# A quarter of the input projection as seven products of quadrants in one first stage, and a thinner projection beside each attention unit

## The reference

```python
h = rmsnorm(x, norm_w)
qa, ka, va, ga, qb, kb, vb, gb = split(h @ w_in)     # 1024, 1024, 1024, 1024, 1024, 128, 128, 1024 columns
qa, ka = rope(rmsnorm(heads(qa))), rope(rmsnorm(heads(ka)))   # 16 heads of 64 each
# A: 8 units; two causal softmax maps of 1024x1024 each, their difference times v (128 wide)
oa = rmsnorm((softmax(q1 @ k1.T) - lam * softmax(q2 @ k2.T)) @ va) * (1 - lam_init)
# B: 16 query heads on 2 key/value heads, window of 128, a learned sink in each softmax
y = concat(oa * silu(ga), ob * silu(gb))
out = x + y @ w_out
```

## Time and profile before

| | us |
|---|---|
| executions shown, two | 1876.48 and 1877.36 |
| median | 1876.92 |
| profiled execution, span of its core | 1877.2 |
| PE busy | 1807.0 |
| DVE busy | 1109.2 |
| ACT busy | 799.8 |
| POOL busy | 439.0 |

### The profile page before, as it was taken

The page is one execution under the profiler, slowest core; times in us unless marked ns, Lnnn a source line. Parts: engine busy times, 40 slices in busy tenths (PEclk is TensorE's granted clock), DMA queues, the critical chain, the costliest instruction groups (busy, mean ns, idle before and its releaser), DMA issues.

```text
span 1877.2 us, 27880 instructions
## 1 busy us (share of the span) xinstructions
PE 1807.0 (96%) x8920; PEld 1507.0 (80%) x8920; DVE 1109.2 (59%) x2255; ACT 799.8 (43%) x2116; POOL 439.0 (23%) x664
## 2 busy tenths in 40 slices
PE   3899999999999999999999999999999889999999
PEld 3788878888788887888878888888888678788887
DVE  5734465665656657566575666758677866333333
ACT  5411354444544445444444444445444554222221
POOL 6512131322313223131231312313223521000000
PEclk9999999999999999999999999999999889999999
DMA  5122222222222222222222222323323544444445
GB/s 201 36 79 73 84 72 78 78 78 78 71 77 77 77 78 71 85 69 87 68 74 86 73 84 74 105 82 83 109 80 98 189 127 122 162 154 161 142 143 177
DMA packets 256504, 184.97 MB, mean 99 GB/s; under 512 B 31136, under 2 KB 227744, under 8 KB 255392
## 3 DMA queue, kind: packets, MB, share of 16 engines
q1 hardware_dynamic: 254352, 183.85, 32.3%
q10 hardware_dynamic: 2064, 0.01, 0.1%
HBM read 138.71 MB, written 45.09 MB: 98 GB/s over the span
## 4 chain that ended last, share of the span: by engine, by line
PE 79%; DVE 9%; issue 4%; DMA 3%; ACT 2%; POOL 2%; SPq 1%; DVEq 0%; ACTq 0%
PE ps_a L854 19%; PE ps_a L856 19%; PE ps_a L855 19%; PE ps_b L938 3%; PE ps_b L856 3%; PE ps_b L854 3%; PE ps_b L855 3%; PE ps_a L898 2%; DVE stage_rows L1124 2%; DMA qkv_sb<-qkv_a_dram 2%; PE ps_a L897 2%; PE ps_b L953 2%; PE ps_b L891 2%; PE ps_b L984 1%; DVE w_lo_sb L1124 1%
## 5 line engine op out<-in xcount | busy, mean ns | idle before, releaser
L854 PE MATMUL ps_a<-hT_hi,w_hi_sb 128*128 128x512 f32 x1696 | 694.1, 409 | 7.2 <-DVE stage_rows L1208 4.5
L856 PE MATMUL ps_a<-hT_hi,w_lo_sb 128*128 128x512 f32 x1696 | 667.4, 394 | 0.0
L855 PE MATMUL ps_a<-hT_lo,w_hi_sb 128*128 128x512 f32 x1696 | 664.1, 392 | 0.0
L1124 DVE TENSOR_TENSOR w_lo_sb<-w_raw_sb,w_hi_sb 128x512 fp32r<-128x512 f32 (+1 forms) x320 | 228.3, 716 | 272.1 <-ACT w_hi_sb L657 270.1
L856 PEld LDWEIGHTS ps_a<-hT_hi,w_lo_sb 128*128 128x128 f32 x1696 | 320.1, 189 | 71.8
L854 PEld LDWEIGHTS ps_a<-hT_hi,w_hi_sb 128*128 128x128 f32 x1696 | 321.2, 189 | 70.2 <-issue 7.2
L855 PEld LDWEIGHTS ps_a<-hT_lo,w_hi_sb 128*128 128x128 f32 x1696 | 321.8, 190 | 58.5
L657 ACT ACTIVATE w_hi_sb<-w_raw_sb 128x512 fp32r<-128x512 f32 (+1 forms) x320 | 197.8, 620 | 226.4 <-DMA w_raw_sb<-in_w_out 95.0
L817 ACT ACTIVATE expd<-ps_a,neg_max 128x256 f32<-128x256 f32 (+7 forms) x128 | 95.1, 743 | 213.3 <-DVE neg_max L1265 211.4
L749 ACT ACTIVATE attention_parts<-ps_b 128x512 fp32r<-128x512 f32 (+3 forms) x160 | 76.9, 521 | 224.2 <-PE ps_b L938 224.0
L1124 DVE TENSOR_TENSOR ps_a<-ps_a,mask 128x128 f32<-128x128 f32 (+2 forms) x192 | 77.5, 417 | 142.2 <-PE ps_a L898 140.8
(11 more groups left out here) (126 smaller groups left out, 2651.6 us busy)
## 6 DMA issues: line engine op xcount, KB each, us to landing
w_raw_sb<-in_w_in SPq DMA_DIRECT2D x200, 256.0 KB, 3.1
w_raw_sb<-in_w_out SPq DMA_DIRECT2D x104, 256.0 KB, 3.1
qkv_a_dram<-stage_rows SPq DMA_DIRECT2D x48, 256.0 KB, 2.4
qkv_sb<-qkv_a_dram SPq DMA_DIRECT2D x64, 192.0 KB, 3.0
x_raw_sb<-in_x SPq DMA_DIRECT2D x8, 1024.0 KB, 7.6
gates_dram<-stage_rows SPq DMA_DIRECT2D x32, 256.0 KB, 2.7
gate_y<-gates_dram SPq DMA_DIRECT2D x128, 64.0 KB, 2.4
y_dram<-gate_y SPq DMA_DIRECT2D x128, 64.0 KB, 2.3
```

What stands on the lines that cost most here:

```text
L854: pe.matmul(dst, a_hi, b_hi, start=start, stop=False)
L855: pe.matmul(dst, a_hi, b_lo, start=False, stop=False)
L856: return pe.matmul(dst, a_lo, b_hi, start=False, stop=stop)
L1124: return dve.tensor_tensor(o, a, b, op)
```

## The change

**Units of kind A.** Their q and k no longer come from `quarter`. A unit beside which an A unit's projection runs has two tiles (v, gate), eight quarters, and `place` puts a whole quarter (both halves, 8 triples) at each even half step and none at the odd ones. Only the v tile is turned, at half steps 8 and 9. This holds for `body(-1)` and for the bodies of units 0 to 6; beside unit 7 and the B units the projection is as before. Scores, exponentials and values are untouched.

**First stage.** The 2048 columns of q and k of all A units, by 1024 tokens, by k of 2048, are one product of 2 by 2 quadrants. It is done with seven products of quadrants in place of eight (sums of quadrants of h before, of w before, and of the results behind). Each of the seven has 16 "tiles" j: k block k of 8, column half c of 2, with four blocks of tokens, so 4 triples; NT = 112 tiles in all (`product_tile`). Tokens lie on the partitions of the result, so it need not be turned. Each engine has a `first_stage(j)`:
- SP loads the weights of tile j+4 (two loads in operations 2 to 5), stores combined weights and finished rows; h itself is stored to DRAM and loaded again at the end of the stage, to become `hT_hi` and `hT_lo`.
- POOL adds or subtracts two weight tiles (`combine_w`, 64 tiles), sums h's quadrants (`sum_h`, 16), adds result parts (`add_row`, 16).
- ACT makes the high part of tile j+2, DVE its low part (`tile_lo`). PE's tile j+2 waits for that.
- DVE adds finished groups out of PSUM (`evacuate`).
- 32 "rows" (128 tokens by 512 columns, 8 heads) are normalised and rotated: at start j of row R ACT squares it, at j+1 DVE sums (`sum_row`) and POOL takes the power (`row_norm`), at j+2 ACT scales its 8 heads (`scale_row`), at j+3 DVE rotates (`turn_row`), at j+4 SP stores. In one DVE `first_stage` the rotation of row R stands ahead of the sum of row R+1. Starts are two tiles apart, in four runs of eight.

The first product begins when four of the eight blocks of x are turned; the other four are turned between tiles 0 to 7. The k and v tiles of B follow the stage, with all their quarters behind it, and rows 25 to 31 run beside them. PE enters `body(-1)` once POOL has cleared `kT_lo`, and POOL does this after the last row has landed in DRAM.

The core of the diff:

```diff
-NQ_IN = 4 * (2 + 4 * (AH + BC))
...
+def place(k, s):
+
+    if k == "A":
+        return s // 8, s % 8 // 2, () if s % 2 else (0, 1)
+    return s // 4, s % 4, (0, 1)
+
...
+def turned_slot(k, s):
+
+    if k == "A":
+        return 0 if s in (8, 9) else None
+    return s // 4 - 1 if s >= 4 and s % 4 < 2 else None
+
...
+NK = KT // 2
+NOP = 7
+NT = NOP * 2 * NK
+SETS = 4
+TWO_LOADS = (2, 3, 4, 5)
...
+N_SLOTS = 3
+N_RING = 16
+
+EVAC_BB = {24 + 2 * n: n for n in range(8)}
+EVAC_V = {56 + 8 * c + r: 4 * c + r for c in range(2) for r in range(4)}
+EVAC_BT = {72 + 2 * n: n for n in range(8)}
+EVAC_H = {88 + 8 * c + r: 4 * c + r for c in range(2) for r in range(4)}
+EVAC_SB = {104 + 8 * c + r: 4 * c + r for c in range(2) for r in range(4)}
+EVAC_G = {8 + 8 * c + r: 4 * c + r for c in range(2) for r in range(4)}
+EVAC_GB = {40 + 8 * c + r: 4 * c + r for c in range(2) for r in range(4)}
...
+ROW_START = ([25 + 2 * n for n in range(8)] + [74 + 2 * n for n in range(8)] + [92 + 2 * n for n in range(8)]
+             + [110 + 2 * n for n in range(8)])
+ROW_AT = {t: R for R, t in enumerate(ROW_START)}
...
+            def load_tile(j):
+
+                op, c, k, m = j // 16, j // NK % 2, j % NK, j % SETS
+                wait(sp, sm["f_lo"], j - SETS + 1)
+                if j - SETS >= 0 and (j - SETS) // 16 in (2, 3):
+                    sp.wait_ge(t_stored[m], 16 * stores_of(j - SETS))
...
+            def store_row(R):
+
+                t, qk, c = ROWS[R]
+                sp.wait_ge(sm["row_done"], R + 1)
+                dst = scr_a[4 * c:4 * c + 4, 1 + t * P:1 + (t + 1) * P, qk * P:(qk + 1) * P].rearrange("a t c -> t a c")
+                done = row_stored[R % N_SLOTS] if R < N_RING else sm["row_parked"]
...
+            def first_stage(j):
+
+                if j + 2 < NT and (j + 2) // 16 in (2, 3):
+                    store_comb(j + 2)
+                if j - 4 in ROW_AT:
+                    store_row(ROW_AT[j - 4])
+                if j + SETS < NT:
+                    load_tile(j + SETS)
...
+            def square_row(R):
...
+                act.activation(row_sq, row_ap(R), ACT.Square).then_inc(sm["row_sq"], 1)
+
+            def scale_row(R):
+
+                act.wait_ge(sm["row_rs"], 3 * R + 3)
+                a = row_ap(R)
+                for n in range(8):
+                    h = slice(n * HD, (n + 1) * HD)
+                    ins = act.activation(a[:, h], a[:, h], ACT.Copy, scale=row_ss(R)[:, n:n + 1])
+                ins.then_inc(sm["row_scaled"], 1)
...
+            def first_stage(j):
+
+                if j + 2 < NT:
+                    tile_hi(j + 2)
...
+                    copy_group(EVAC_G[j], g_part, j)
+                if j in EVAC_GB:
+                    copy_group(EVAC_GB[j], gb_part, j)
+                if z_unit(j):
+                    z_high(*z_unit(j))
+                if j - 2 in ROW_AT:
+                    scale_row(ROW_AT[j - 2])
+                if j in ROW_AT:
+                    square_row(ROW_AT[j])
+                if j in H_SPLIT:
+                    h_high(H_SPLIT[j])
...
                 u = s // 4
+                first_stage(NT + 2 * s)
+                first_stage(NT + 2 * s + 1)
...
                     if d:
-                        quarter(d, u, s % 4, 0, before)
+                        q, halves = place(d["kind"], s)[1:]
+                        for b in halves[:1]:
+                            quarter(d, u, q, b, before)
...
                         turn_o(back2, it, first)
                     if d:
-                        quarter(d, u, s % 4, 1, before)
+                        for b in halves[1:]:
...
+            def product_tile(j):
+
+                g, k, op = j // NK, j % NK, j // 16
+                if k == 0 and g == 1:
+                    pe.wait_ge(sm["x_ev_dve"], 3 * NR)
+                    pe.wait_ge(sm["x_ev_act"], NR)
+                elif k == 0 and g >= 2:
+                    by, n = evacs_before(g - 2)
+                    pe.wait_ge(sm["ev_" + by], n)
+                pe.wait_ge(sm["f_lo"], j + 1)
+                if g % 2 == 0 and k % 2 == 0:
+                    pe.wait_ge(sm["z_lo_ready"], 4 * op + k // 2 + 1)
+                for r in range(4):
+                    t = slice(k * 512 + r * P, k * 512 + (r + 1) * P)
+                    mm = three((ps_a, ps_b)[g % 2][:, r, :], z_hi[op % 2][:, t], z_lo[op % 2][:, t],
+                               w_hi[:, j % 4, :], w_lo[:, j % 4, :], k == 0, k == NK - 1)
+                mm.then_inc(sm["f_used"], 1)
+
...
+            def tile_lo(j):
+                dve.wait_ge(sm["f_hi"], j + 1)
+                tt(w_lo[:, j % 4, :], w_sets[j % SETS][0], w_hi[:, j % 4, :].bitcast(F32), ALU.subtract)\
+                    .then_inc(sm["f_lo"], 1)
...
+            def add_part(n, dst, src, g):
+
+                dve.wait_ge(sm["f_used"], NK * (g + 1))
+                tt(dst, bank(g, n % 4), src, ALU.add).then_inc(sm["ev_dve"], 1)
...
+                    n = R % 8
+                    if R >= N_SLOTS:
+                        dve.wait_ge(row_stored[R % N_SLOTS], 16 * (R // N_SLOTS))
+                    if R < 8:
+                        dve.wait_ge(sm["ev_act"], n + 1)
...
+            def sum_row(R):
+                dve.wait_ge(sm["row_sq"], R + 1)
+                if R >= 3:
+                    dve.wait_ge(sm["row_scaled"], R - 2)
+                dve.tensor_reduce(row_ss(R), row_sq.rearrange("p (g c) -> p g c", g=8), AX, ALU.add)\
+                   .then_inc(sm["row_ss"], 1)
+
+            def turn_row(R):
+
+                t, qk, _ = ROWS[R]
+                a = row_ap(R)
+                x4, t4 = (b.rearrange("p (g f c) -> p g f c", g=8, f=2) for b in (a, row_tmp))
+                cs, sn = (b[qk].rearrange("p (r c) -> p r c", r=NR)[:, t, :] for b in (rope_c, rope_s))
+                dve.wait_ge(sm["row_scaled"], R + 1)
+                wait(dve, sm["row_done"], R)
+                for f in range(2):
+                    ins = tt(t4[:, :, f, :], x4[:, :, 1 - f, :],
+                             sn[:, f * HALF:(f + 1) * HALF].unsqueeze(1).to_broadcast([P, 8, HALF]), ALU.mult)
+                ins.then_inc(sm["row_chain"], 1)
+                dve.wait_ge(sm["row_chain"], 2 * R + 1)
+                x3 = a.rearrange("p (g c) -> p g c", g=8)
+                tt(x3, x3, cs.unsqueeze(1).to_broadcast([P, 8, HD]), ALU.mult).then_inc(sm["row_chain"], 1)
...
+            def first_stage(j):
+
+                if j + 2 < NT:
+                    tile_lo(j + 2)
...
+                evacuate(j)
+                if z_unit(j):
+                    z_low(*z_unit(j))
+                if j - 3 in ROW_AT:
+                    turn_row(ROW_AT[j - 3])
+                if j - 1 in ROW_AT:
+                    sum_row(ROW_AT[j - 1])
...
+            def combine_w(j):
+                op, m = j // 16, j % SETS
+                pool.wait_ge(f_in[m], 16 * set_loads(j))
+                a, b = w_sets[m]
+                pool.tensor_tensor(a, a, b, ALU.add if op == 3 else ALU.subtract).then_inc(sm["f_comb"], 1)
...
+            def add_row(n):
+
+                R = 8 + n
+                if R < 16:
+                    pool.wait_ge(sm["ev_dve"], 16 + n + 1)
+                    pool.wait_ge(sm["ev_act"], 8 + n + 1)
...
+            def row_norm(R):
+                pool.wait_ge(sm["row_ss"], R + 1)
+                inv_rms(row_ss(R), row_mean[:, :], row_ss(R), 2, sm["row_rs"], 3 * R)
...
+            def first_stage(j):
+
+                if j + 3 < NT and (j + 3) // 16 in TWO_LOADS:
+                    combine_w(j + 3)
+                if j - 1 in EVAC_BT:
+                    add_row(EVAC_BT[j - 1])
+                if j - 1 in EVAC_H:
+                    add_row(8 + EVAC_H[j - 1])
+                if j - 1 in ROW_AT:
+                    row_norm(ROW_AT[j - 1])
...
+            pool.wait_ge(sm["row_parked"], 16 * (len(ROWS) - N_RING))
+            for c in range(2):
+                pool.memset(kT_lo[c][half_rows[1 - c], :].bitcast(F32), 0.0).then_inc(sm["k_zeros"], 1)
+                pool.wait_ge(sm["k_zeros"], c + 1)
```

More of the change, by code:

```diff
@@ L124, in uses_of @@
         turned = []
-        if s % 4 < 2 and s >= 4:
-            p = s // 4 - 1
-            if proj and tile_desc((proj, 0), p)["turned"]:
+        p = turned_slot(proj, s) if proj else None
+        if p is not None:
+            if tile_desc((proj, 0), p)["turned"]:
                 turned.append(("PT", p, s % 2))
@@ L354, in proj_tile, with quarter_now, quarter_slot, last_step @@
             else:
-                before = tile_desc((kind(first), it), 3)
+                k = kind(first)
+                before = tile_desc((k, it), 1 if k == "A" else 3)
             return d, u, before
+        def quarter_now(it, first, s):
+            k = proj_kind(first + 1)
+            p, q, halves = place(k, s)
+            u = it * (2 if k == "A" else 4) + tile_number(k, 1, p)
+            return u * 4 + q, 0 in halves
+        def quarter_slot(first, s):
```

(41 more changed lines are left out.)

592 lines of the change are left out of this document (429 added, 163 removed).

## The result

The changed kernel takes 2073.96 us (2073.35 to 2074.57), 1.1045 times the time of before, interval 1.1024 to 1.1066. The forecast was 1953, so the sign was right and the size wrong by 121 us, outside the range. The profiled execution has a span of 2072.6 us.

What follows compares the result with a forecast made beforehand. PE's work was taken to bound the kernel: 1877.2 + 239.0 for unit 0's later start - 336.7 in seven units = 1779.5, plus 110 of unit waits and 63 in the first stage, 1952.5, forecast 1953 us; range 1885 to 2005.

Steps and rivals of the forecast that it cites:

- PE's own work: Whole kernel: PE loses 192 matmuls and 128 transposes; with no wait at all the time would be 1779.5 us.
- The thin units: Units 0 to 6: each loses 48.1 us of PE time and gains 15.7 of waiting, 83.9 us a unit.
- 14.7 us of waiting before the second scores: Units 0 to 6: the empty half step leaves the softmax between both scores uncovered, 14.7 us a unit.
- The first stage: Seven products with rows: waits for rows, port, splits of h and B tile sum to 63 us, between 25 and 95.
- A row's period is 7.2 us: First stage: sum, POOL's operations, scaling, rotation and wakes take 7.2 us a row against PE's 5.46, 1.75 lost.
- the ring: First stage: rotation of row R precedes sum of row R+1 on DVE, closing a loop over DVE, POOL and ACT.
- 4 us for the splits of h: First stage: splits of h on DVE and POOL beside rows 8 to 23 add 4 us.
- the port's row: First stage: trace of DVE splits held up by POOL, 2.13 us for 0.68; applied to rows 8 to 15, 8 us.
- A: First stage: rows cost nothing and it runs at PE's pace; time 1889.5 us, within 2%; chance 0.15.
- C: Units 0 to 6: second scores aren't late and rows cost nothing; faster, time about 1791 us; chance 0.04.
- B: Units 0 to 6: PE's clock falls behind 14 gaps, 32 us, time 1985; with 35 gaps 2033; chance 0.14.
- D: First stage: loads bind it, DMA allowing only 200 GB/s in operations 2 and 3; 33 us more, 1985; chance 0.07.

Runs made afterwards that it cites:

- e1: Changed kernel, but DVE rotates row R and sums row R+1 before it splits tile j+2; 2039.1 us, ratio 1.0863.
- e8: Changed kernel with the rows' square, sum, scaling and rotation cut to 8 of 512 columns; 1982.9 us, ratio 1.0561.
- e5: Changed kernel with each projection quarter cut in token halves, half 0 beside the even half step, half 1 beside the odd; 2054.9 us, ratio 1.0944.
- e10: e5 with q and k of the next step turned ahead of the values' products in odd half steps; 2057.7 us, ratio 1.0956.
- e12: Changed kernel with a whole projection quarter at each odd half step and none at the even ones; 2317.1 us, ratio 1.2344.
- e13: e10 plus ring opened, loads before row store, POOL's h sums paced, and q and k splits ahead of second softmax's exponential and combination; 1982.8 us.

## Why the forecast was wrong

**PE's own work** was right: 8600 matmuls, and the part from unit 7 on within 2.1 us.

**The thin units** were right in mechanism and in sum (84.7 us for 83.9), the sum partly by luck. I had 14.7 us of waiting before the second scores and 1.0 elsewhere, with gaps of 1.5 to 2.4. Measured are 11.3 us a unit, in gaps of up to 1.6, of which 4.7 are right before the second scores and 6.6 before a transpose whose bank DVE has yet to free (`turn_o` or the turned tile). Those transposes stand between the first and the second scores, and the softmax still decides when the second scores begin:

```profile
918.98 0.28 PE L1236 MATMUL ps_a<-attention_parts,q_hi_lo 128*128 128x256 f32 x1
...
921.25 0.33 PE L1312 MATMUL ps_b<-ident,o_sb 128*128 128x128 f32 x1 [1.44 <-DVE attention_parts L1474]
...
921.43 0.19 ACT L1144 ACTIVATION_READ_ACCUMULATOR expd<-ps_a,neg_max 128x1 f32 x1
...
921.67 0.50 PE L1235 MATMUL ps_a<-attention_parts,q_hi_lo 128*128 128x512 f32 x1
```

They start 0.05 us behind that read in 49 of the 56 steps and 0.17 to 0.29 behind it in the other seven. So the wait for a bank lies inside the path that I had forecast and doesn't add to it. The waiting was 4.4 us a unit less than forecast, and PE's own time 5.2 more (73.4 for 68.2), of which the clock is 2.9 (20 us in the seven units) and the rest is open: two errors that offset each other.

**The first stage is the step that failed**, by 116.6 of the 120 us between the sum of 1952.5 and the span of 2072.6. Its terms:
- *"A row's period is 7.2 us; DVE's other work fits in the 4.2 us in which it waits."* It doesn't fit, since `tile_lo` waits for ACT's `tile_hi`, which stands behind ACT's scaling. Measured 9.8 to 10.9 in rows 0 to 7; e1, which makes the sentence true, gives 7.8 to 8.0. (Rows 9 to 26 are 8.8 to 16.0 apart and in e1 still 7.5 to 16.2; what adds to the ring there is only in part priced.) I had followed DVE's order and not ACT's. The scaling itself, 2.02 for 2.0, was right. All the rows are worth 92 us (e8), where my terms for them, without the 4 for the splits of h, came to 59.
- *"4 us for the splits of h"*, and nothing else without rows. Measured in e8: 88 us. The largest are operations 1 (19 us, twelve POOL sums in one run beside DVE's splits, tables and `z_low`), 5 (22) and 2 (12). I had the port's row, and applied it to rows 8 to 15 only, not to `sum_h`, the longest run on POOL. I never listed POOL's work by tile.
- *The clock.* The sum held no term for it inside the stage. My own gaps per row, 1.75 us, were under those of the earlier trace rows. Once they were 2 to 5 us, each cost about 2 more: 46 us of work lost in the stage.

**The rivals.** A (rows cost nothing) is refuted. C too. B named the right mechanism: in the units the clock fell 12 times, eleven of them in steps 5 to 7, and cost 20 us of work, where B had 14 falls and 32 us. It didn't lengthen the forecast unit only because there was less waiting. B left out the stage, where it fell 24 times. My sign for it, a mean under 0.97, came true (0.953), and most of that is the stage. D took 200 GB/s for what DMA allows; operation 3, with two loads and a store a tile, ran at 265 GB/s and 3.01 us a tile, so all its losses are 4.5 us there, not half of 33. The range's upper end allowed for one surprise at a time, and three came together.

## What to carry to other kernels

A ring through several engines holds every instruction that stands between its members in each engine's order; walk all the queues, SP's too, before saying that other work "fits in the wait". List by time what each engine does in a new stage: a long run on POOL beside DVE's splits is a term, though no engine is busy by half. Where a queue is thin, moving its work (e5, e10, e12, e13) exchanges one late chain for another.
